# A working buffer of a fused transformer kernel, and the offsets in it, at multiples of 64 bytes

## The reference

```python
for l in range(DEPTH):                      # 2
    if l == N_A:
        shared = nsa_shared_kv(x, ...)      # keys and values: compressed, selected, window
    mem_k, mem_v = (rmsnorm(mem, g_mem[l]) @ w_mem_kv[l])
    h = rmsnorm(x, g_mix[l])
    x = x + (gla_layer_mix if l < N_A else nsa_layer_mix)(h, ...)   # both also attend to mem
    x = x + conv_ffn(rmsnorm(x, g_ffn[l]), w_up[l], conv_w[l], conv_b[l], w_down[l])
x = rmsnorm(x, g_final)
...
```

## Time and profile before

| | us |
|---|---|
| median of 3 runs | 2185.58 |
| lowest, highest | 2179.38, 2186.24 |
| the profiled execution | 2182.03 |
| its span, first to last instruction | 2180.3 |
| PE busy | 2060.7 |
| DVE busy | 1037.6 |
| ACT busy | 838.7 |
| POOL busy | 132.3 |
| mean granted TensorE clock | 0.973 |

### The profile page before, as it was taken

The page is one execution under the profiler, slowest core; times in us unless marked ns, Lnnn a source line. Parts: engine busy times, 40 slices in busy tenths (PEclk is TensorE's granted clock), DMA queues, the critical chain, the costliest instruction groups (busy, mean ns, idle before and its releaser), DMA issues. The chain is left out here.

```text
span 2180.3 us, 27474 instructions
## 1 busy us (share of the span) xinstructions
PE 2060.7 (95%) x10545; PEld 1638.2 (75%) x10545; DVE 1037.6 (48%) x1555; ACT 838.7 (38%) x1301; POOL 132.3 (6%) x136
## 2 busy tenths in 40 slices
PE   7999879999999999889999999999998899999998
PEld 5686637888878787556788878778786678888786
DVE  7421742544443452653554543344655347565632
ACT  4533153332332454652432332344653334333323
POOL 0000001000000100440000000100041010000001
PEclk9999799999999999899999999999999999999999
DMA  4420012333322251002333323233110033323221
GB/s 163 133 78 1 1 39 95 108 97 96 96 90 96 66 153 56 1 1 78 97 94 99 94 90 105 59 97 87 49 40 2 1 97 97 106 87 106 88 96 39
DMA packets 135401, 167.69 MB, mean 77 GB/s; under 512 B 28307, under 2 KB 102536, under 8 KB 135304
## 3 DMA queue, kind: packets, MB, share of 16 engines
q1 hardware_dynamic: 134598, 166.12, 24.5%
q10 hardware_dynamic: 705, 0.25, 0.0%
HBM read 164.24 MB, written 2.10 MB: 76 GB/s over the span
## 5 line engine op out<-in xcount | busy, mean ns | idle before, releaser
L178 PE MATMUL bank<-h_hi,w_hi 128*128 128x512 f32 (+1 forms) x2256 | 874.7, 388 | 19.7 <-DVE h_lo L315 6.7
L180 PE MATMUL bank<-h_hi,w_lo 128*128 128x512 f32 (+1 forms) x2256 | 873.0, 387 | 0.0
L179 PE MATMUL bank<-h_lo,w_hi 128*128 128x512 f32 (+1 forms) x2256 | 873.0, 387 | 0.0
L142 DVE TENSOR_TENSOR w_lo<-raw,w_hi 128x1024 fp32r<-128x1024 f32 x306 | 371.7, 1224 | 779.4 <-ACT w_hi L136 778.1
L136 ACT CAST w_hi<-raw 128x1024 fp32r<-128x1024 f32 x306 | 318.6, 1048 | 759.7 <-PE bank L178 751.3
L178 PEld LDWEIGHTS bank<-h_hi,w_hi 128*128 128x128 f32 x2256 | 425.0, 188 | 114.5 <-issue 15.6
L180 PEld LDWEIGHTS bank<-h_hi,w_lo 128*128 128x128 f32 x2256 | 424.7, 188 | 86.4
L179 PEld LDWEIGHTS bank<-h_lo,w_hi 128*128 128x128 f32 x2256 | 425.0, 188 | 84.9
L259 POOL TENSOR_TENSOR keep<-keep 128x512 f32<-128x512 f32 x30 | 41.9, 1395 | 1492.8 <-ACT keep L252 1491.1
L165 PE MATMUL bank<-level,ident 128*128 128x512 f32 x174 | 82.2, 621 | 10.7 <-ACT h_words L2590 3.8
L1198 ACT COPY keep<-bank 128x512 f32<-128x512 f32 x88 | 51.8, 589 | 75.6 <-PE bank L180 74.4
(11 more groups left out here) (441 smaller groups left out, 1776.3 us busy)
## 6 DMA issues: line engine op xcount, KB each, us to landing
raw<-in_w_up SPq DMA_DIRECT2D x176, 256.0 KB, 3.0
raw<-in_w_down SPq DMA_DIRECT2D x44, 512.0 KB, 3.2
raw<-in_w_ffn_up SPq DMA_DIRECT2D x88, 256.0 KB, 3.0
raw<-in_w_mix_in SPq DMA_DIRECT2D x24, 512.0 KB, 3.7
raw<-in_w_ffn_down SPq DMA_DIRECT2D x22, 512.0 KB, 3.4
raw<-in_w_mem_kv SPq DMA_DIRECT2D x16, 512.0 KB, 5.7
raw<-in_a_w_in SPq DMA_DIRECT2D x16, 512.0 KB, 3.8
raw<-in_a_w_out SPq DMA_DIRECT2D x8, 512.0 KB, 6.0
```

Source lines behind the costliest of these rows:

```text
L142: dve.tensor_tensor(k.w_lo[n % RING][:, :], k.raw[n % RING][:, :], k.w_hi[n % RING][:, :].bitcast(F32), ALU.subtract)\
L178: a = pe.matmul(out, sh, mh, start=first, stop=False)
L179: pe.matmul(out, sh, ml, start=False, stop=False)
L180: c = pe.matmul(out, sl, mh, start=False, stop=last)
```

## The change

The constant `KEEP` grows from 15400 to 15408 words; `dist_cmp` is made 132 words wide, of which the first 124 are used as before; and every offset in `keep` that was 8 words past a multiple of 16 is raised by 8. No instruction is added, removed or moved on any engine: the lists of the two built programs read the same on PE, DVE, ACT, POOL and SP.

```diff
-    mprobT = k.carve(13352, (2, 512))
+    mprobT = k.carve(13360, (2, 512))
...
-    k.qkv = k.carve(3080, (12, 512))
-    k.zT = k.carve(9224, (4, 512))
-    k.sbq, k.sbk, k.sbv = k.carve(11272, (2, 512)), k.carve(12296, (2, 512)), k.carve(13320, (4, 256))
-    k.gab, k.decay_all, k.decay_row = k.carve(14344, (32,)), k.carve(14376, (8,)), k.carve(14384, (8,))
-    k.last_decay = k.carve(14392, (H, C))
-    small = lambda i: k.carve(14408 + 16 * i, (C, H))
+    k.qkv = k.carve(3088, (12, 512))
+    k.zT = k.carve(9232, (4, 512))
+    k.sbq, k.sbk, k.sbv = k.carve(11280, (2, 512)), k.carve(12304, (2, 512)), k.carve(13328, (4, 256))
+    k.gab, k.decay_all, k.decay_row = k.carve(14352, (32,)), k.carve(14384, (8,)), k.carve(14392, (8,))
+    k.last_decay = k.carve(14400, (H, C))
+    small = lambda i: k.carve(14416 + 16 * i, (C, H))
...
-    old_sq, k.sq = k.sq, k.carve(9224, (8, 512))
+    old_sq, k.sq = k.sq, k.carve(9232, (8, 512))
...
-    S = [k.carve(5128 + i * 512, (H, P)) for i in range(2)]
-    vn = [k.carve(6152 + i * 512, (H, P)) for i in range(2)]
+    S = [k.carve(5136 + i * 512, (H, P)) for i in range(2)]
+    vn = [k.carve(6160 + i * 512, (H, P)) for i in range(2)]
...
-KEEP = 15400
+KEEP = 15408
...
-        k.dist, k.dist_cmp = sb("dist", [P, 512]), sb("dist_cmp", [P, 4 * 31])
+        k.dist, k.dist_cmp = sb("dist", [P, 512]), sb("dist_cmp", [P, 132])[:, 0:4 * 31]
```

## The result

| | us |
|---|---|
| before, median (6 runs) | 2185.6, from 2179.38 to 2186.72 |
| changed, median (6 runs) | 2224.68, from 2224.14 to 2228.54 |
| ratio, 95% interval | 1.0186, 1.0175 to 1.0197 |
| changed, the profiled execution and its span | 2224.51, 2222.8 |

The changed kernel is 1.9% slower, well outside the forecast range. The page of after first: PE is busy for 45.9 us more than in the earlier trace rows, with the same number of instructions, and a weight load still takes 188 ns. The ring's products hold most of it.

The account below looks back on a forecast made before the run. The prediction took PE's products to bound the dense stages and engine handoffs the sparse ones. PE 0, DVE 0, ACT 0.1, POOL 0.14, DMA 0 made about 0.3 us gained: 2183.8 less 0.3, 2183.5 us, range 2178 to 2190.

Parts of the forecast that it names:

- What bounds the kernel: Dense stages: PE bound, products start every 0.22 to 0.23 us, 39 ns cover left per load; sparse stages: engines alternate.
- What the change does to the addresses: Only addresses change: `keep` becomes 64-byte aligned, everything behind it slides 64 bytes; `xT`, `h_hi`, `h_lo`, `rstd`, `dist` stay.
- PE: 0 us: Products and weight loads on PE: unaligned reads from `keep` cost nothing, so aligning them gains 0 us.
- The rival of the weight ring: `w_hi`, `w_lo` 64 past a multiple of 128 load a quarter slower, outgrowing 39 ns cover: 54 us lost, 2238 us; chance 0.02.
- DVE and ACT: Vector and activation lines touching `keep` and `pad`: alignment gains 0 us on DVE, 0.1 us on ACT.
- POOL: 0.14 us: L259's adds ahead of the norm sums fall from 1292 to about 1270 ns; last add of six chains: 0.14 us gained.
- DMA: 0 us: Transfers of `x` into `keep` and of the weight ring: taken as 0, bound of 0.6 us either way.
- The clock and the sum: Sum: about 0.3 us gained. Clock rival: eight more low-clock places lose 6.8 us, 2190.3 us; chance 0.02.
- The signs: What the after profile should show: medians kept within 3 ns, L259 about 1270 ns, `x` wait 8.8 to 9.8 us.
- the dense stretches changed in length at equal clock: Sign of a wrong forecast: the dense PE stretches change length while the clock is equal; no size given.
- the products of L178 still start every 0.23 us: Sign of a right forecast: spacing of L178's products on PE stays at 0.23 us.

Follow-up runs that it names:

- all64: The kernel before with 64 unused bytes ahead of `xT`, so every tensor from there on moves by 64 bytes: 2185.48 us, beside 2184.86 for the kernel before.
- ring64: The kernel before with 64 unused bytes between `tail` and the weight ring, so only the ring moves: 2224.08 us against 2184.86 for the kernel before.
- lo64both: The kernel before with `h_lo` 64 bytes further from `h_hi` and `w_lo` 64 further from `w_hi`: 2210.33 us, beside 2180.85 for the kernel before.
- aligned_ring256: The changed kernel with 192 unused bytes ahead of the ring, its distance from `h_hi` now 256: 2182.49 us against 2184.11 for the kernel before, ratio 0.9995.

## Why the prediction was wrong

**What bounds the kernel.** Right: the dense stages are bound by the products, and only they moved. But I read "a product starts every 0.22 to 0.23 us" and didn't ask what 512 columns should take. The trace of before had the answer. Products of 256 columns start 120.3 ns apart and those of 512 columns 226.8 ns: 106.5 ns for 256 more columns, one column per cycle at 2.4 GHz, and so 213 ns for 512. The sums of squares of L271 are plain float32, and their records follow each other every 429 or 430 ns, (1.88 - 0.59) / 3, in before:

```profile
373.99 1.88 PE L271 MATMUL bank<-keep,ones 128*128 128x512 f32 x4
```

That is twice 215 ns, as if each record streamed its 512 columns twice with next to nothing between; no run shows that it does. A ring product took 226.7 ns, so by the first sum some 13 ns of each weren't streaming even before, an estimate of 86 us over 6576 products. There was a cost to be made larger, with no cover over it.

**What the change does to the addresses.** Right, and the decisive line stands in it: everything behind `keep` slides by 64 bytes while `h_hi` and `h_lo` do not move. I looked at each address past 64 and 128, and not at the distance between two operands of one product.

**PE: 0 us.** This is the term that failed; it measured +42.0 us. The rows under it were the wrong ones: L165, L271 and L1675 are plain float32 products. These are indeed insensitive: after the change, at another distance, L271 still has its 592 ns in every record, and its records still follow each other every 429 or 430 ns.

```profile
L271 PE MATMUL bank<-keep,ones x24: 592/592/592, 380.0 to 2205.1; 128*128 128x512 f32 x24
```

The ring's products have float32r operands, and in before nearly all of them stood at one distance, so the trace of before had no second value to compare. There was one hint: the products of `w_hi` with the compression's `kv_hi`, whose tiles start at many places, mostly follow each other at 115 to 127 ns, where the other 256-wide ones nearly all hold 120 (these products have 68 weight columns and not 128, so it was no more than a hint).

**The rival of the weight ring.** It named the right tensors and the right sign, and missed by its trigger. I let it cost nothing until a load outgrew 39 ns of cover, and gave it 0.02. The loads stayed at 188 ns, and the products were spaced 6.5 ns wider all the same. "Cover" counted from a load's duration presumes that the load and the stream above it don't slow each other. The Trainium skill presumes the same (TensorE: Matmul & The Clock Gate, Step-by-step: what each phase is for): PE has two independent read ports. "Loading the next tile's weights doesn't steal SBUF read bandwidth from the running matmul." all64 and ring64 fit that badly: the ring at one and the same address costs 0 or 6.5 ns per product, by where the moving operand stands. They don't refute it, since that it is these two reads that meet isn't shown; lo64both leaves it open.

**DVE and ACT.** Right. L1263 has 750/752/756 ns and L1198 587/589/593, both for 88 instructions; L295 stays at 747 and L308 at 621 where it was 620.

**POOL: 0.14 us.** Wrong: alignment gained nothing, and the vector width of 64 bytes in the Trainium skill (GPSIMD: programming the Q7 cores, Q7 Core Specifications) explains nothing here. L259 is now aligned and takes 1295 ns in the median, where it took 1292. What the 23 ns to L2603 come from wasn't tried; it isn't the alignment. L259's mean fell from 1395 to 1295 ns, because three adds of 2332 ns are gone, and PE's wait for it from 1.8 to 0.6 us:

```profile
L259 POOL TENSOR_TENSOR keep<-keep x30: 1288/1295/1307, 360.8 to 2201.5; 128x512 f32<-128x512 f32 x30
...
  PE bank L268: 0.6, 2
```

In aligned_ring256 `keep` is aligned too, and both are back (maximum 2328, PE's wait 1.8 us), so neither comes from the alignment. The long adds come from a meeting with DVE. In before each of the three begins 0.04 us after a subtraction of L142 has begun on DVE. The subtraction takes its 1.23 us and the add 1.04 us more than usual. In after the same three adds begin 0.10 or 0.11 us ahead of the subtraction. Now the add is quick and the subtraction takes 2.28 us. Whichever begins second is held up. The first of the three subtractions, before and then after:

```profile
357.94 1.23 DVE L142 TENSOR_TENSOR w_lo<-raw,w_hi 128x1024 fp32r<-128x1024 f32 x1 [4.22 <-ACT w_hi L136]
```

```profile
363.60 2.28 DVE L142 TENSOR_TENSOR w_lo<-raw,w_hi 128x1024 fp32r<-128x1024 f32 x1 [4.37 <-ACT w_hi L136]
```

PE's shorter wait has nothing to do with these: each is the third add of its chain, and the fourth begins some 10 us after its end. PE waits less because its products ahead of the sums now end closer to the last add; in aligned_ring256, at the pace of before, the wait is that of before.

**DMA: 0 us.** Right: PE still waits 9.3 us for `x`, and a transfer takes 5.2 us to land where it took 5.1.

**The clock and the sum.** The mean granted clock is 0.971 after and 0.973 before, and the stages that grew are at full clock in both; the clock took no part. Without the PE term the forecast agrees with the measurement, which can't resolve a gain of 0.3 us: aligned_ring256 has all edits and lies at 0.9995 (0.9984 to 1.0006), where about 0.9999 was forecast.

**The signs.** One of the signs of being wrong came true: the dense stretches changed in length at equal clock. Another could not have shown the loss: "the products of L178 still start every 0.23 us" holds for 226.8 and for 233.3 ns alike. A sign has to be as fine as the effect that would sink the forecast, and here 1 ns of spacing is 6.6 us.

## What to carry to other kernels

Inserting a few bytes ahead of a tensor moves every tensor behind it: look at the distances between operands of one product as well as at the addresses. For float32r products of 512 columns, keep the moving and the stationary tensors at the same place modulo 256 bytes, and check it after every change to the layout; an assert in the code would have caught this. (Products of 256 columns were quickest elsewhere in these runs.) A load that is shorter than the product above it isn't thereby free: compare the spacing of products with the columns they stream before you call anything covered.

## What the runs showed of the hardware

- The spacing of 128x512 float32r products with 128x128 weights depends on the distance between the moving and the stationary tensor, modulo 256 bytes: 226.8 ns at 0, from 229.1 to 234.2 at the seven other multiples of 32, 232.4 at 4, 237.1 at 4 short of a period. Moving both together changes nothing (226.8 in all64). The wider spacing stays while DVE, ACT, POOL and the transfers are idle (233.3 ns from 1813 us of after).
- The sign counts: 64 past costs 6.5 ns and 64 short 2.3 ns, and exchanging the operands exchanges the two.
- For 128x256 products it is the other way: 120.3 ns at 0 and 116.1 at 64 past. What is best for one width isn't for another.
- At 16 bytes the same loop ran at 233.3 ns in one stretch and at 226.7 in another, and changed only where PE had paused.
- Plain float32 products of 512 columns (L271) take 592 ns a record, and start 429 or 430 ns apart, at either distance.
- On DVE, ACT and POOL, an operand in SBUF that starts 32 past a multiple of 64 bytes costs nothing in these lines against one that starts at a multiple: L1263, L1198, L295, L308 and L259 stay within 3 ns of where they were.
- A POOL add of 128x512 (L259) and a DVE subtraction of 128x1024 (L142) hold each other up: the one that begins second took 1.04 to 1.05 us longer, the add 2.33 us in before and the subtraction 2.28 us in after.
